# One encoder step on one core: attention groups written out, the softplus of both pairs of heads together, magnitudes on VectorE, last rows stored by quarters

## The chip, the core and the metric

The kernel runs on one core of a Trainium2 chip. The metric is the device time of one execution in microseconds (us). The core's engines are TensorE (PE: matmuls and transposes; PEld is its weight load), VectorE (DVE), ScalarE (ACT), GpSimd (POOL) and SyncE (SP), whose queue (SPq) starts most of the transfers. They run side by side and wait for each other through semaphores.

## The reference

```
layer 0: x = x + gate1 * (attention(norm(x)) @ w_o);   x = x + gate2 * swiglu(norm(x))
layer 1: x = x + gate1 * pool_mixer(norm(x));          x = x + gate2 * swiglu(norm(x))

z       = (q @ k.T) * HEAD_DIM ** -0.5                  # per head, strictly causal
ls_neg  = log_sigmoid(-z)                               # = -softplus(z)
log_1m  = where(causal, ls_neg, 0)
later   = cumsum(log_1m, reverse=True) - log_1m
weights = where(causal, exp(z + ls_neg + later), 0)
out     = weights @ v
```

There are 256 new frames of one prompt and 16 new frames of each of 8 running streams (384 tokens), a width of 2048, 16 heads of 128, 512 cached keys and values for each stream, a feed-forward width of 5632, and everything is in 32-bit floats. The changed code is attention in layer 0 and the last stage, which returns x as rows.

## The kernel before

The order of the work is written out by hand: each engine has its own program, and counting semaphores connect them. x lies in SBUF with features on partitions. The weights come in pieces of 1 MB. ACT and VectorE split each piece into a high and a low part, and TensorE makes three products of them (lines 1458 to 1460). This makes up nearly the whole kernel. Between the projections of q, k and v and the output projection stands attention.

Attention takes the heads in four groups of four. Each engine runs one loop over the groups. Within a group the heads form two pairs for the new frames' own scores ("self"), and the streams form two halves of four for the scores against the cache ("past"). A group goes so:

- TensorE turns q and k (line 1628), ACT copies qT, VectorE copies kT (line 1192), and TensorE makes the self scores of all four heads (lines 1722 to 1724).
- For each of the 8 streams b, TensorE turns the cached keys (`turn_keys(b)`, line 1639). ACT copies two heads of them and VectorE the other two (`keys_out(b)`, lines 761 and 1199). TensorE makes the past scores (`past_scores(b)`, line 1652), ACT copies them out (`scores_row(b)`, line 767), TensorE turns them back (`turn_scores(b)`, line 1660), and VectorE stores them (`scores_out(b)`, line 1205).
- In between, each self pair and each past half needs softplus(z) = max(z, 0) + log(1 + exp(-|z|)). ACT makes |z|, exp and log one after another in one buffer, `e_buf` (lines 744, 748, 750), and VectorE adds max(z, 0) (lines 1229 and 1252). Exp and log lie in different tables of ACT, and a change between them is an ACT_TABLE_LOAD. TensorE then sums along the keys with a triangular matrix (`self_sums`, line 1698; `past_sums`, lines 1667 and 1668), VectorE subtracts the sums, ACT takes exp, and TensorE multiplies with the values (`self_values`, `past_values`, line 1680). Past outputs leave through `out_row` (ACT, line 771) and `turn_out` (line 1687).

Each piece of the cache has one of four buffers. SP loads a new one when `turn_keys` or `past_values` has used the old one (line 371).

At the end of the kernel, after the last residual addition (lines 1046 to 1054), TensorE turns all of x with 48 transposes (line 1895). VectorE and ACT copy them into `yrow`, and SP stores it with three transfers (line 479).

Of the kernel before, what the change touches and what calls it, by code (L numbers as in the profile page):

```python
# [23 lines left out]
ALU = mybir.AluOpType  # L24
# [77 lines left out]
def encoder_step(nc, x_prompt, x_sample, c_prompt, c_sample, cache_k, cache_v, state_pool,  # L102
# [5 lines left out]
    with ctx:  # L108
# [76 lines left out]
        e_buf = at(R2 + 8192, "e_buf", [P, 2, 512])  # L185
        sp_buf = at(R2 + 12288, "sp_buf", [P, 2, 512])
# [8 lines left out]
        z_rows = [at(H0 + 14 * TOK * 4, "z_row0", [P, 512]), at(H0 + (KT + 14) * TOK * 4, "z_row1", [P, 512])]  # L195
# [30 lines left out]
        front_free, back_free, kturn_done, qkT_done, qT_ready, kT_ready = sem("front_free"), sem("back_free"), sem("kturn_done"), sem("qkT_done"), sem("qT_ready"), sem("kT_ready")  # L226
        zself_done, zself_taken = sem("zself_done"), sem("zself_taken")
# [54 lines left out]
        def unit(W, n):  # L282

            return W + n // 4, n % 4

# [33 lines left out]
        def _(sp):  # L319
# [155 lines left out]
            sp.wait_ge(y_act, 6)  # L475
            sp.wait_ge(y_dve, 6)
            for t in range(TT):
                dst = y_prompt[0, t * P:(t + 1) * P] if t < 2 else y_sample.rearrange("b t n -> (b t) n")
                sp.dma_start(dst, yrow[:, t]).then_inc(y_stored, 16)
            sp.wait_ge(y_stored, 16 * TT)  # L480
# [70 lines left out]
        def _(act):  # L551
# [189 lines left out]
            def softplus_step(z, i):  # L741

                if i == 0:
                    step.mark(act.activation(e_buf[:], z, ACT.Abs))
                    return
                act.wait_ge(act_step, step.value())
                if i == 1:
                    step.mark(act.activation(e_buf[:], e_buf[:], ACT.Exp, scale=-1.0))
                else:
                    act.activation(e_buf[:], e_buf[:], ACT.Ln, bias=1.0).then_inc(ln_ready, 1)  # L750

            with loop(act, 0, HG, {step: 8}) as g:
                act.wait_ge(qkT_done, g + 1)
# [19 lines left out]
                def self_rest(p, i):  # L773
                    if i == 0:
                        act.wait_ge(zself_taken, 2 * g + p + 1)
                        if p:
                            act.wait_ge(sp_ready, 4 * g + 1)
                    softplus_step(zs_self[:, 2 * p:2 * p + 2], i)

# [11 lines left out]
                def past_rest(q, i):  # L791
                    if i == 0:
                        act.wait_ge(zpast_taken, 8 * g + 4 * q + 4)
                        act.wait_ge(sp_ready, 4 * g + 2 + q)
                    softplus_step(half(zs_past, q), i)

# [15 lines left out]
                act.wait_ge(of_ready, g + 1)  # L812
                act.activation(h_hi[:, ds(g * 4, 4), PROMPT:TOK], o_f[:], ACT.Copy).then_inc(ofhi_ready, 1)
# [112 lines left out]
            for i in range(1, 12, 2):  # L926
                t, q = i % TT, i // TT
                act.wait_ge(yT_done, i + 1)
                act.activation(yrow[:, t, q * 512:(q + 1) * 512], bank[:, i % 6], ACT.Copy).then_inc(y_act, 1)
# [5 lines left out]
        def _(dve):  # L935
# [254 lines left out]
            with loop(dve, 0, HG, {step: 8}) as g:  # L1190
                dve.wait_ge(kturn_done, g + 1)
                dve.tensor_copy(kT[:], bank[:, 4:8, 0:TOK]).then_inc(kT_ready, 1)
# [22 lines left out]

                def self_scores(p):

                    dve.wait_ge(zself_done, g + 1)
                    pair = slice(2 * p, 2 * p + 2)
                    dve.scalar_tensor_tensor(zs_self[:, pair], bank[:, pair, :], SCALE, mask[:].unsqueeze(1).to_broadcast([P, 2, 512]),  # L1220
                                             ALU.mult, ALU.min).then_inc(zself_taken, 1)

                def self_sp(p):
# [5 lines left out]
                    dve.scalar_tensor_tensor(sp_buf[:], zs_self[:, 2 * p:2 * p + 2], 0.0, e_buf[:], ALU.max, ALU.add).then_inc(sp_ready, 1)  # L1229
# [40 lines left out]
                keys_out(0); self_scores(0)  # L1270
                keys_out(1); self_scores(1); self_sp(0)
# [12 lines left out]
                dve.wait_ge(opast_taken, 4 * g + 4)  # L1284
                own()
                dve.tensor_tensor(o_f[:], o_f[:], o_new[:], ALU.add).then_inc(of_ready, 1)
                dve.wait_ge(ofhi_ready, g + 1)
                k = ds(g * 4, 4)
                dve.tensor_tensor(h_lo[:, k, PROMPT:TOK], o_f[:], h_hi[:, k, PROMPT:TOK].bitcast(f32), ALU.subtract).then_inc(o_split, 1)
# [65 lines left out]

            def dense_chunk(W, c, r, last=False):
# [5 lines left out]
                for s in range(4):  # L1362
                    if not last:
                        dense(W, 12 + s)
                    down_add(4 * W + 9 + s, s, r, 1)

# [79 lines left out]
            for i in range(0, 12, 2):  # L1446
                t, q = i % TT, i // TT
                dve.wait_ge(yT_done, i + 1)
                dve.tensor_copy(yrow[:, t, q * 512:(q + 1) * 512], bank[:, i % 6]).then_inc(y_dve, 1)

# [4 lines left out]
        def _(pe):  # L1455
# [48 lines left out]
            def to_features(W, n, b0, act_h, act_l, k0, start, stop, second_half=None):  # L1504
# [3 lines left out]
                for k in range(4):  # L1508
                    if k == 2 and second_half:
                        pe.wait_ge(h_ready, second_half)  # L1510
# [111 lines left out]
            with pe.Fori(0, HG) as g:  # L1622
                pe.wait_ge(qk_loaded, 48 * g + 48)
                for i, free, done in ((0, front_free, qkT_done), (1, back_free, kturn_done)):
# [5 lines left out]
                    last.then_inc(done, 1)  # L1630

                def turn_keys(b):
                    pe.wait_ge(kv_loaded[b % 4], 64 * g + (16 * (b // 4) + 16))
                    for i, taken in ((0, keys_act), (1, keys_dve)):
                        if b:
                            pe.wait_ge(taken, 8 * g + b)
                        for h in (2 * i, 2 * i + 1):
# [80 lines left out]
                pe.wait_ge(kT_ready, g + 1)  # L1718
                turn_keys(0)
                pe.wait_ge(qT_ready, g + 1)  # L1720
                for h in range(4):
# [200 lines left out]
```

## Time and profile before

| | us |
|---|---|
| median of 3 runs | 3508.49 |
| lowest and highest run | 3506.6 and 3509.36 |
| the profiled execution's own time | 3510.57 |
| its span, first to last instruction | 3507.7 |

A profile comes from one execution, here one with 3507.7 us between its first and last instruction and 2.9 us around them. The page of the profile gives each engine's busy time. A window gives the same for a stretch, with the clock that TensorE was granted (1.00 is 2.4 GHz, 0.50 is 1.2 GHz). In a timeline the brackets hold the idle time before an instruction and what ended it.

### The profile page before, as it was taken

The page shows a single profiled execution, that of the slowest core. Times are in us where ns is not written, and L with a number is a line of the kernel's source. Part 1 is how long each engine was busy: PE and PEld are TensorE (multiplying, and loading weights), DVE is VectorE, ACT ScalarE, POOL GpSimd, SP SyncE. Part 2 cuts the span into 40 slices and gives each one's busy share as a digit, 9 for nine tenths or more (in the row PEclk, how much of TensorE's full clock was granted, in tenths as well). Part 3 has the DMA queues.
Part 4 walks back from the last instruction along what each step waited for, and adds up shares of the span by engine and source line. Part 5 has one row for each costly group of instructions (what it writes and reads, how often), then busy time and mean ns, then how long its engine had stood idle before and what let it go on. Part 6 is the DMA issues. An engine that isn't in the chain of part 4 may idle for free.

```text
span 3507.7 us, 48646 instructions
## 1 busy us (share of the span) xinstructions
PE 3316.0 (95%) x20405; PEld 2992.5 (85%) x20405; DVE 2076.4 (59%) x1782; ACT 1339.3 (38%) x1020; POOL 140.8 (4%) x141
## 2 busy tenths in 40 slices
PE   7999997887989999999999999878999999999998
PEld 4677775555978999999999999757999999999998
DVE  3487883444887777677776777675444443344443
ACT  3344444555444433444334443334222232322221
POOL 0000000000000000000000000010000000000000
PEclk9999998899999999999999999878999999999999
DMA  9776775676655555555555555463334333333331
GB/s 352 263 271 239 252 245 179 241 246 233 229 179 204 192 180 182 201 203 191 179 183 200 203 191 179 160 210 123 131 120 131 126 125 129 122 131 120 129 123 59
DMA packets 325244, 645.13 MB, mean 184 GB/s; under 512 B 11561, under 2 KB 14129, under 8 KB 324401
## 3 DMA queue, kind: packets, MB, share of 16 engines
q1 hardware_dynamic: 317984, 630.29, 52.6%
q10 hardware_dynamic: 7194, 13.91, 1.1%
q8 instruction: 47, 0.77, 0.1%
q14 instruction: 19, 0.16, 0.0%
HBM read 630.47 MB, written 13.69 MB: 184 GB/s over the span
## 4 chain that ended last, share of the span: by engine, by line
PE 86%; DVE 4%; DMA 4%; ACT 3%; issue 1%; SPq 1%; ACTq 0%; DVEq 0%
PE bank L1458 23%; PE bank L1460 22%; PE bank L1459 22%; PE bank L1537 3%; PE bank L1485 3%; PE bank L1539 3%; PE bank L1538 3%; DMA raw<-in_w_ada 3%; PE bank L1494 1%; PE bank L1667 1%; PE bank L1470 1%; PE bank L1639 1%; DVE w_lo L944 1%; PE bank L1668 1%; PE bank L1698 1%
## 5 line engine op out<-in xcount | busy, mean ns | idle before, releaser
L944 DVE TENSOR_TENSOR w_lo<-raw,w_hi 128x2048 fp32r<-128x2048 f32 x324 | 741.3, 2291 | 905.5 <-ACT w_hi L565 905.5
L565 ACT ACTIVATE w_hi<-raw 128x2048 fp32r<-128x2048 f32 x324 | 618.0, 1914 | 1379.9 <-PE bank L1460 1186.0
L1458 PE MATMUL bank<-h_hi,w_hi 128*128 128x384 f32 x3136 | 1064.2, 339 | 37.1 <-DVE h_lo L1023 23.3
L1460 PE MATMUL bank<-h_hi,w_lo 128*128 128x384 f32 x3136 | 1053.1, 336 | 0.0
L1459 PE MATMUL bank<-h_lo,w_hi 128*128 128x384 f32 x3136 | 1052.0, 335 | 0.0
L1458 PEld LDWEIGHTS bank<-h_hi,w_hi 128*128 128x128 f32 x3136 | 592.1, 189 | 83.0 <-issue 75.6
L1459 PEld LDWEIGHTS bank<-h_lo,w_hi 128*128 128x128 f32 x3136 | 592.4, 189 | 0.0
L1460 PEld LDWEIGHTS bank<-h_hi,w_lo 128*128 128x128 f32 x3136 | 591.7, 189 | 0.0
L1458 PE MATMUL bank<-act_hi,w_hi 128*128 128x384 f32 x1408 | 472.7, 336 | 0.0
L1460 PE MATMUL bank<-act_hi,w_lo 128*128 128x384 f32 x1408 | 470.5, 334 | 0.0
L1459 PE MATMUL bank<-act_lo,w_hi 128*128 128x384 f32 x1408 | 470.5, 334 | 0.0
L949 DVE TENSOR_TENSOR w_mid<-raw,w_top 128x2048 f32<-128x2048 f32 x144 | 329.0, 2285 | 11.5 <-ACT w_top L572 11.5
L951 DVE TENSOR_TENSOR w_top<-w_mid 128x2048 bf16<-128x2048 f32 x144 | 330.1, 2292 | 5.0
L572 ACT ACTIVATE w_top<-raw 128x2048 bf16<-128x2048 f32 x144 | 273.7, 1901 | 155.2 <-PE bank L1460 128.6
L1458 PEld LDWEIGHTS bank<-act_hi,w_hi 128*128 128x128 f32 x1408 | 264.3, 188 | 4.8 <-POOL act_lo L535 4.8
L1459 PEld LDWEIGHTS bank<-act_lo,w_hi 128*128 128x128 f32 x1408 | 264.3, 188 | 0.0
L1460 PEld LDWEIGHTS bank<-act_hi,w_lo 128*128 128x128 f32 x1408 | 264.3, 188 | 0.0
L535 POOL TENSOR_TENSOR act_lo<-act_f,act_hi 128x384 fp32r<-128x384 f32 x88 | 88.0, 1018 | 2728.7 <-ACT act_hi L839 2727.6
L1537 PE MATMUL bank<-w_hi,h_hi 128*128 128x512 f32 x480 | 192.5, 401 | 2.6 <-DVE w_lo L944 2.6
L1539 PE MATMUL bank<-w_hi,h_lo 128*128 128x512 f32 x480 | 187.8, 391 | 0.0
L1538 PE MATMUL bank<-w_lo,h_hi 128*128 128x512 f32 x480 | 187.6, 391 | 0.0
L1051 DVE SCALAR_TENSOR_TENSOR x<-bank,modT,x 128x256 f32<-128x256 f32 x384 | 158.4, 474 | 0.0
(219 smaller groups left out, 2564.8 us busy)
## 6 DMA issues: line engine op xcount, KB each, us to landing
raw<-in_w_ada SPq DMA_DIRECT2D x192, 1024.0 KB, 5.6
raw<-in_w_gate SPq DMA_DIRECT2D x88, 1024.0 KB, 5.2
raw<-in_w_up SPq DMA_DIRECT2D x88, 1024.0 KB, 5.2
raw<-in_w_down SPq DMA_DIRECT2D x88, 1024.0 KB, 5.1
raw<-in_w_qkv SPq DMA_DIRECT2D x40, 1024.0 KB, 5.2
raw<-in_cache_k SPq DMA_DIRECT2D x32, 1024.0 KB, 5.4
raw<-in_cache_v SPq DMA_DIRECT2D x32, 1024.0 KB, 6.8
raw<-in_w_o SPq DMA_DIRECT2D x16, 1024.0 KB, 5.0
```

Of the source, the lines that this page charges most:

```text
L565: act.activation(w_hi[:, s], raw[:, s], ACT.Copy).then_inc(hi_ready, 1)
L572: act.activation(w_top[:, s, 0], raw[:, s], ACT.Copy).then_inc(hi_ready, 1)
L944: dve.tensor_tensor(w_lo[:, s], raw[:, s], w_hi[:, s].bitcast(f32), ALU.subtract).then_inc(lo_ready, 1)
L949: dve.tensor_tensor(w_mid[:, s], raw[:, s], w_top[:, s, 0], ALU.subtract).then_inc(lo_ready, 1)
L951: dve.tensor_tensor(w_top[:, s, 1], w_mid[:, s], mid_top(s), ALU.subtract).then_inc(top_rest, 1)
L1051: step.mark(dve.scalar_tensor_tensor(xv, ps[:, k, 0:PROMPT], mod[:, k, 0:1], xv, ALU.mult, ALU.add))
L1458: pe.matmul(out, w, a, start=start, stop=False)
L1459: pe.matmul(out, w, al, start=False, stop=False)
L1460: return pe.matmul(out, wl, a, start=False, stop=stop)
L1537: pe.matmul(out, h_hi[:, kt, cols], w_hi[:, s, k], start=(kt == 0), stop=False)
L1538: pe.matmul(out, h_hi[:, kt, cols], w_lo[:, s, k], start=False, stop=False)
L1539: last = pe.matmul(out, h_lo[:, kt, cols], w_hi[:, s, k], start=False, stop=(kt == KT - 1))
```

## The change

1. The loops over the four groups are written out on TensorE, ACT and VectorE, so every wait names a constant.
2. kT is copied in two halves. The first starts when two heads' keys are turned, and turn_keys(0) waits for each half of the banks by itself. The self scores are signalled by pairs.
3. |z| is made on VectorE (`magnitude`), for the second self pair in a second buffer, `e_second`. ACT then takes exp of both self pairs and later log of both (`exp_part`, `log_part`).
4. TensorE does self_sums(0) after turn_scores(2) (it was after turn_scores(0)), self_sums(1) after turn_scores(3) (after turn_scores(2)), and past_sums(0) after past_scores(7) (before it).
5. A group's closing sum and split of the past outputs (`out_sum`, `out_lo`; on ACT `out_hi`) run at the start of the next group.
6. In the last chunk of the last feed-forward, the down projection makes x by quarters of 512 features. Each of the first three quarters is turned half-way through the next quarter's matmuls and the last one after the end. Each quarter is copied and stored by itself, so there are 12 stores of 256 KB instead of 3 of 1 MB.

```diff
-            with loop(act, 0, HG, {step: 8}) as g:
-                act.wait_ge(qkT_done, g + 1)
+            for g in range(HG):
+                act.wait_ge(qkT_done, 2 * g + 2)
                 act.activation(qT[:], bank[:, 0:4, 0:TOK], ACT.Copy).then_inc(qT_ready, 1)
...
+                def exp_part(i):
+
+                    e = e_second if i == 1 else e_buf
+                    act.wait_ge(abs_ready, 4 * g + i + 1)
+                    act.activation(e[:], e[:], ACT.Exp, scale=-1.0).then_inc(exp_ready, 1)
+
+                def log_part(i):
+
+                    e = e_second if i == 1 else e_buf
+                    act.wait_ge(exp_ready, 4 * g + i + 1)
+                    act.activation(e[:], e[:], ACT.Ln, bias=1.0).then_inc(ln_ready, 1)
...
-                keys_out(0); self_rest(0, 0); self_rest(0, 1)
-                keys_out(1); self_rest(0, 2); scores_row(0)
-                keys_out(2); scores_row(1); self_rest(1, 0)
-                keys_out(3); self_rest(1, 1); scores_row(2); self_rest(1, 2)
-                keys_out(4); scores_row(3)
-                keys_out(5); scores_row(4); self_w(0); past_rest(0, 0)
-                keys_out(6); past_rest(0, 1); scores_row(5); past_rest(0, 2)
-                keys_out(7); scores_row(6); scores_row(7); self_w(1); past_w(0)
-                past_rest(1, 0); past_rest(1, 1); past_rest(1, 2)
                 self_hi(0); out_row(0); past_w(1); self_hi(1); out_row(1)
...
+                keys_out(0); keys_out(1); exp_part(0)
+                scores_row(0); keys_out(2); exp_part(1)
+                scores_row(1); log_part(0); keys_out(3); log_part(1)
+                scores_row(2); keys_out(4)
+                scores_row(3); keys_out(5)
+                scores_row(4); self_w(0); exp_part(2); keys_out(6); log_part(2)
+                scores_row(5); keys_out(7)
+                scores_row(6); self_w(1); scores_row(7); past_w(0)
+                exp_part(3); log_part(3)
...
+            for g in range(HG):
+                for i in range(2):
+                    dve.wait_ge(kturn_done, 2 * g + i + 1)
+                    dve.tensor_copy(kT[:, 2 * i:2 * i + 2], bank[:, 4 + 2 * i:6 + 2 * i, 0:TOK]).then_inc(kT_ready, 1)
...
+                def magnitude(i):
+
+                    if i < 2:
+                        z, e = zs_self[:, 2 * i:2 * i + 2], (e_buf, e_second)[i]
+                        dve.wait_ge(zself_taken, 2 * g + i + 1)
+                    else:
+                        z, e = half(zs_past, i - 2), e_buf
+                        dve.wait_ge(zpast_taken, 8 * g + 4 * (i - 2) + 4)
+                        dve.wait_ge(sp_ready, 4 * g + (1 if i == 2 else 3))
+                    dve.scalar_tensor_tensor(e[:], z, -1.0, z, ALU.mult, ALU.max).then_inc(abs_ready, 1)
...
+                if g:
+                    out_sum(g - 1)
+                keys_out(0)
+                if g:
+                    out_lo(g - 1)
+                self_scores(0)
+                keys_out(1); magnitude(0); self_scores(1); magnitude(1)
                 keys_out(2); scores_out(0)
-                keys_out(3); self_t(0); scores_out(1); self_sp(1)
-                keys_out(4); scores_out(2)
-                keys_out(5); scores_out(3); self_t(1)
+                keys_out(3); scores_out(1); self_sp(0)
+                keys_out(4); scores_out(2); self_t(0); self_sp(1)
+                keys_out(5); scores_out(3); magnitude(2); self_t(1)
                 keys_out(6); scores_out(4); past_sp(0)
-                keys_out(7); scores_out(5); past_t(0); scores_out(6)
-                scores_out(7)
-                dve.wait_ge(o_split, g + 1)
+                keys_out(7); scores_out(5); past_t(0); scores_out(6); scores_out(7)
+                magnitude(3)
...
+            def rows_out(q):
+
+                for t in (0, 2):
+                    dve.wait_ge(yT_done, TT * q + t + 1)
+                    dve.tensor_copy(yrow[:, t, q * 512:(q + 1) * 512], bank[:, y_bank(q) + t]).then_inc(y_dve, 1)
...
-                turn_keys(2); past_scores(1); turn_scores(0); self_sums(0)
+                turn_keys(2); past_scores(1); turn_scores(0)
...
+            def turn_rows(q):
+
+                pe.wait_ge(residual_taken, R_END - 3 + q)
+                for t in range(TT):
+                    for k in range(4):
+                        last = pe.transpose(bank[:, y_bank(q) + t, k * P:(k + 1) * P], x[:, 4 * q + k, t * P:(t + 1) * P], ident[:])
+                    last.then_inc(yT_done, 1)
```

How the written order moves, at three places. First ACT in attention, from the second self pair's magnitude on (before): `e_buf<-zs_self` is |z|, `e_buf<-e_buf` after it is exp and then log, `z_row` is a copy of scores.

```order
L744 ACTIVATE e_buf<-zs_self 128x1024
L758 REGISTER_ALU
L761 ACTIVATE keys<-bank 128x1024
L746 REGISTER_ALU
L748 ACT_TABLE_LOAD
L748 ACTIVATE e_buf<-e_buf 128x1024
L764 REGISTER_ALU
L767 ACTIVATE z_row_109<-bank 128x512
L746 REGISTER_ALU
L750 ACT_TABLE_LOAD
L750 ACTIVATE e_buf<-e_buf 128x1024
L758 REGISTER_ALU
```

Now, from the first exp of a group on:

```order
L775 ACT_TABLE_LOAD
L775 ACTIVATE e_buf<-e_buf 128x1024
L765 ACTIVATE z_row_110<-bank 128x512
L759 ACTIVATE keys<-bank 128x1024
L775 ACTIVATE e_second<-e_second 128x1024
L765 ACTIVATE z_row_111<-bank 128x512
L781 ACT_TABLE_LOAD
L781 ACTIVATE e_buf<-e_buf 128x1024
L759 ACTIVATE keys<-bank 128x1024
L781 ACTIVATE e_second<-e_second 128x1024
```

|z| has left ACT, exp of one pair and exp of the other share one table, log of both shares the next, and key copies stand between them.

Second, TensorE in attention, from past_scores(1) on (before). `sp_buf,tri` and `sp_buf,ones` are self_sums, `ident,raw` is turn_keys, `keys,qT` is past_scores, `ident,z_row` is turn_scores.

```order
L1652 MATMUL bank<-keys,qT 32x512 x4
L1660 MATMUL bank<-ident,z_row_109 128x128 x4
L1692 ISA
L1696 REGISTER_ALU
L1698 MATMUL bank<-sp_buf,tri 128x512
L1699 MATMUL bank<-sp_buf,ones 128x128
L1698 MATMUL bank<-sp_buf,tri 128x512
L1699 MATMUL bank<-sp_buf,ones 128x128
L1636 REGISTER_ALU
L1639 MATMUL bank<-ident,raw 128x128 x16
```

Now, from turn_scores(2) on:

```order
L1692 MATMUL bank<-ident,z_row_110 128x128 x4
L1730 MATMUL bank<-sp_buf,tri 128x512
L1731 MATMUL bank<-sp_buf,ones 128x128
L1730 MATMUL bank<-sp_buf,tri 128x512
L1731 MATMUL bank<-sp_buf,ones 128x128
L1671 MATMUL bank<-ident,raw 128x128 x16
L1684 MATMUL bank<-keys,qT 32x512 x4
L1692 MATMUL bank<-ident,z_row_111 128x128 x4
L1730 MATMUL bank<-sp_buf,tri 128x512
L1731 MATMUL bank<-sp_buf,ones 128x128
```

Self_sums(0) stands two streams later, and self_sums(1) one stream after it.

Third, the end of TensorE's program. Before, where `ident,x` are the transposes of x:

```order
L1458 MATMUL bank<-act_hi,w_hi 128x384
L1459 MATMUL bank<-act_lo,w_hi 128x384
L1460 MATMUL bank<-act_hi,w_lo 128x384
L1884 REGISTER_ALU
L1884 COMPARE_AND_BRANCH
L1895 MATMUL bank<-ident,x 128x128 x48
```

Now, half-way through the last quarter's matmuls:

```order
L1486 MATMUL bank<-act_lo,w_hi 128x384
L1487 MATMUL bank<-act_hi,w_lo 128x384
L1860 MATMUL bank<-ident,x 128x128 x12
L1485 MATMUL bank<-act_hi,w_hi 128x384
L1486 MATMUL bank<-act_lo,w_hi 128x384
L1487 MATMUL bank<-act_hi,w_lo 128x384
```

The transposes of three quarters stand among the matmuls of the next quarter, 12 at each place, and 12 are left for the end.

## Rows read from the trace of the kernel before

**Rows 1.** the page's part on busy time: us, share of the span, instructions.

```profile
PE 3316.0 (95%) x20405; PEld 2992.5 (85%) x20405; DVE 2076.4 (59%) x1782; ACT 1339.3 (38%) x1020; POOL 140.8 (4%) x141
```

**Rows 2.** windows over attention: length, busy per engine, clock, DMA share, GB/s.

```profile
542.77:865.17 322.40, 259.83 (x2368) 179.30 (x2368) 132.46 (x183) 173.74 (x186) 0.00 (x0) 0.91 0.64 224
625.26:706.56 81.30, 65.70 (x592) 45.18 (x593) 33.60 (x47) 43.91 (x47) 0.00 (x0) 0.90 0.68 234
654.00:657.00 3.00, 1.09 (x9) 0.52 (x5) 1.34 (x2) 2.89 (x4) 0.00 (x0) 1.00 0.90 287
657.00:660.00 3.00, 3.00 (x6) 1.49 (x7) 1.64 (x3) 0.00 (x0) 0.00 (x0) 0.60 0.93 285
```

**Rows 3.** waits of PE in attention: total us, times, longest.

```profile
PE bank L1667 <- DVE later L1258: 16.0, 8, 3.0
PE bank L1639 <- ACT keys L761: 10.8, 8, 1.7
...
PE bank L1639 <- DVE kT L1192: 7.8, 4, 2.0
PE bank L1698 <- DVE sp_buf L1229: 7.6, 4, 1.9
```

**Rows 4.** ACT's groups in attention: busy us, mean ns, idle before.

```profile
L750 ACT ACT_TABLE_LOAD x16 | 20.5, 1283 | 0.3
L767 ACT ACTIVATE z_row<-bank 128x512 f32<-128x512 f32 x32 | 18.9, 590 | 37.2 <-PE bank L1652 37.2
...
L744 ACT ACTIVATE e_buf<-zs_self 128x1024 f32<-128x1024 f32 x8 | 8.4, 1052 | 21.1 <-DVE zs_self L1220 21.1
```

**Rows 5.** VectorE's groups in attention, same columns.

```profile
L1199 DVE COPY keys<-bank 128x1024 f32<-128x1024 f32 x32 | 39.1, 1222 | 44.2 <-PE bank L1639 44.2
...
L1258 DVE TENSOR_TENSOR later<-later,sp_buf 128x256 f32<-128x256 f32 x24 | 10.2, 425 | 0.8
```

**Rows 6.** timeline of the second group: start, us, engine, line, wait before.

```profile
628.13 1.76 DVE L1192 COPY kT<-bank 128x1536 f32<-128x1536 f32 x1
...
630.02 3.43 PE L1639 MATMUL bank<-ident,raw 128*128 128x128 f32 x16 [1.93 <-DVE kT L1192]
...
641.53 1.28 ACT L750 ACT_TABLE_LOAD   x1
...
641.57 1.97 PE L1639 MATMUL bank<-ident,raw 128*128 128x128 f32 x16 [1.67 <-ACT keys L761]
642.83 1.06 ACT L750 ACTIVATE e_buf<-e_buf 128x1024 f32<-128x1024 f32 x1
...
643.92 1.22 DVE L1229 SCALAR_TENSOR_TENSOR sp_buf<-zs_self,e_buf 128x1024 f32<-128x1024 f32 x1 [2.62 <-ACT e_buf L750]
...
644.52 1.06 PE L1652 MATMUL bank<-keys,qT 128*32 128x512 f32 x8 [0.98 <-ACT z_row L767]
...
675.23 2.08 PE L1667 MATMUL bank<-sp_buf,tri 128*128 128x512 f32 x2 [2.98 <-DVE later L1258]
```

**Rows 7.** timeline, the second half of the values' loads.

```profile
686.50 2.99 SPq L371 DMA_DIRECT2D raw<-in_cache_v  x4
```

**Rows 8.** the cache loads' line: from issue to landing.

```profile
DMA to landing us min/median/max: 4.9/5.6/12.9
```

**Rows 9.** timeline of the end.

```profile
3491.53 0.69 DVE L1054 TENSOR_TENSOR x<-x,tmp_s 128x512 f32<-128x512 f32 x1
...
3492.27 5.46 PE L1895 MATMUL bank<-ident,x 128*128 128x128 f32 x48 [3.08 <-DVE x L1054]
...
3497.77 0.60 ACT L929 ACTIVATE yrow<-bank 128x512 f32<-128x512 f32 x1 [0.28 <-PE bank L1895]
3498.43 1.79 SPq L479 DMA_DIRECT2D out<-yrow  x3
```

**Rows 10.** windows over the last feed-forward and the last stores.

```profile
2460.00:3489.00 1029.00, 1029.00 (x5938) 1028.88 (x5936) 421.00 (x419) 286.48 (x189) 40.29 (x40) 1.00 0.37 119
3499.00:3507.00 8.00, 0.00 (x0) 0.00 (x0) 0.00 (x0) 0.00 (x0) 0.00 (x0) 0.62 0.95 393
```

More of the change, by code:

```diff
@@ L194, in encoder_step @@
         keys = at(R1 + 47104, "keys", [P, 2, 4, 512])
-        z_rows = [at(H0 + 14 * TOK * 4, "z_row0", [P, 512]), at(H0 + (KT + 14) * TOK * 4, "z_row1", [P, 512])]
+        z_rows = [at(H0 + (KT + 12) * TOK * 4 + 2048 * i, f"z_row{i}", [P, 512]) for i in range(2)]
         o_row = at(R1 + 18432, "o_row", [P, 2, 512])
@@ L924, in _ @@
             dense_chunk(W_FFN1 + 3 * (CHUNKS - 1), 2 * CHUNKS - 1, last=True)
[L926 to L929, printed above, removed]
+            for q in range(4):
+                act.wait_ge(yT_done, TT * q + 2)
+                act.activation(yrow[:, 1, q * 512:(q + 1) * 512], bank[:, y_bank(q) + 1], ACT.Copy).then_inc(y_act, 1)
         @block.vector
@@ L1283, in _ @@
                 dve.memset(tmp_s[:, 0, 2:3], 0.0).then_inc(back_free, 1)
[L1284 to L1289, printed above, removed]
+            out_sum(HG - 1)
+            out_lo(HG - 1)
             own()
@@ L1365, in dense_chunk @@
                     down_add(4 * W + 9 + s, s, r, 1)
+                    if last:
+                        rows_out(s)
             with loop(dve, 0, CHUNKS - 1, {step: 4 * ADD}) as c:
@@ L1508, in to_features @@
                 for k in range(4):
+                    if k == 2 and rows_of is not None:
+                        turn_rows(rows_of)
                     if k == 2 and second_half:
@@ L1619, in _ @@
             ada_turn(ADA_O - 1, 7)
-            with pe.Fori(0, HG) as g:
+            for g in range(HG):
                 pe.wait_ge(qk_loaded, 48 * g + 48)
@@ L1629, in _ @@
                                                 tok[:, i, t, h * HD:(h + 1) * HD], ident[:])
-                    last.then_inc(done, 1)
+                        if h % 2:
+                            last.then_inc(done, 1)
                 def turn_keys(b):
@@ L1724, in _ @@
                     last = pe.matmul(bank[:, h, 384:512], kT[:, h, 2 * P:3 * P], qT[:, h, 2 * P:3 * P], start=True, stop=True)
-                last.then_inc(zself_done, 1)
+                    if h % 2:
+                        last.then_inc(zself_done, 1)
                 turn_keys(1); past_scores(0)
-                turn_keys(2); past_scores(1); turn_scores(0); self_sums(0)
+                turn_keys(2); past_scores(1); turn_scores(0)
                 turn_keys(3); past_scores(2); turn_scores(1)
-                turn_keys(4); past_scores(3); turn_scores(2); self_sums(1)
-                turn_keys(5); past_scores(4); turn_scores(3)
+                turn_keys(4); past_scores(3); turn_scores(2); self_sums(0)
+                turn_keys(5); past_scores(4); turn_scores(3); self_sums(1)
                 turn_keys(6); past_scores(5); turn_scores(4)
-                turn_keys(7); past_scores(6); turn_scores(5); past_sums(0)
-                past_scores(7); turn_scores(6); turn_scores(7)
+                turn_keys(7); past_scores(6); turn_scores(5)
+                past_scores(7); past_sums(0); turn_scores(6); turn_scores(7)
                 self_values(0)
@@ L1816, in mixed_chunk, with dense_chunk @@
                 down_rest(W, 16, r)
-            def dense_chunk(W, c, r, hr):
+            def turn_rows(q):
+                pe.wait_ge(residual_taken, R_END - 3 + q)
+                for t in range(TT):
+                    for k in range(4):
+                        last = pe.transpose(bank[:, y_bank(q) + t, k * P:(k + 1) * P], x[:, 4 * q + k, t * P:(t + 1) * P], ident[:])
+                    last.then_inc(yT_done, 1)
+            def dense_chunk(W, c, r, hr, last=False):
                 pe.wait_ge(residual_taken, r - 1)
@@ L1883, in _ @@
             norm_stats(3)
-            with pe.Fori(0, CHUNKS) as c:
+            with pe.Fori(0, CHUNKS - 1) as c:
                 dense_chunk(W_FFN1 + c * 3, c + CHUNKS, R_FFN1 + c * 4, 8)
-            for i in range(12):
-                t, q = i % TT, i // TT
-                if i == 0:
-                    pe.wait_ge(residual_taken, R_END)
-                if i >= 6:
-                    pe.wait_ge(y_act if i % 2 else y_dve, (i - 6) // 2 + 1)
-                for k in range(4):
-                    last = pe.transpose(bank[:, i % 6, k * P:(k + 1) * P], x[:, 4 * q + k, t * P:(t + 1) * P], ident[:])
-                last.then_inc(yT_done, 1)
+            dense_chunk(W_FFN1 + 3 * (CHUNKS - 1), 2 * CHUNKS - 1, R_FFN1 + 4 * (CHUNKS - 1), 8, last=True)
+            turn_rows(3)
 INPUTS = ["x_prompt", "x_sample", "c_prompt", "c_sample", "cache_k", "cache_v", "state_pool", "w_ada",
```

93 lines of the change are left out of this document (45 added, 48 removed).

## The prediction

> **What bounds the kernel now.** I read the page's busy times first. TensorE is busy 95% of the span [rows 1], so in most stages its matmuls set the end and only work taken from them counts. The page's slices show less in few places; attention is one. A window over it, from the first transpose of q to the last of the outputs, has 322.4 us with TensorE busy for 259.8 and a mean clock of 0.91 [rows 2]. So 62.6 us there are waits, and 0.09 x 2 x 322.4 = 58 us pass at 1.2 GHz, which costs up to half of itself, 29 us. Work at full clock is then 259.8 - 29 = 231 us, or 57.7 for each of the four groups; the group in the second row takes 81.3.
>
> The waits come next. The longest kinds are TensorE's for the past sums (16.0), for ACT's key copies (10.8), for kT (7.8) and for the self sums (7.6) [rows 3]. All but kT lead to ACT, which makes |z|, exp and log in one row with table loads: 16 loads stand before a log alone, each 1283 ns [rows 4]. The timeline shows how: ACT's load begins at 641.53 and its log at 642.83, VectorE's sum waits 2.62 for it, TensorE waits 1.67 for the key copy queued between them and 0.98 for the scores' copy; later it waits 2.98 for the past sums' operand [rows 6]. What the waits do to the clock is in two windows: in the 3 us from 654 TensorE is busy for 1.09 us, and in the next 3 the clock's mean is 0.60, at work all the time [rows 2].
>
> **The change, part by part.** ACT loses four |z| a group, 4 x 1.05 = 4.2 us [rows 4], and table loads: by the written order it has 9 a group before, and 7 in the first and 6 in the other groups now, so 11 fewer in all. A load costs ACT 1.28 and the log starts 0.02 after it ends [rows 6], so 11 are 14.3 us of ACT, some 3.6 a group. The Trainium skill (ScalarE: Activation LUTs, "What ACT_TABLE_LOAD costs") adds about 1.38 us of draining to each load, which would make 29 us of them; the rows show no such gap, so 14.3 stands. VectorE gains four magnitudes a group at the 1.22 us of its like [rows 6], 4.9 us, and it has room: busy 132 of 322 [rows 2].
>
> What counts is where TensorE still waits. I laid the new order out at full clock with the durations of the rows: 1.8 us to turn a stream's keys, 1.0 for its scores [rows 6], 1.22 for a key copy, 3 x 0.43 for the three additions of the past sums [rows 5], 0.59 for a scores' copy [rows 4], and 0.1 to 0.3 for each hand-over. Group two onwards:
> - turn_keys(0): 1.93 before [rows 6]. Half of kT takes an estimated 0.95 of the 1.76 and starts six transposes earlier: 0.7 now.
> - turn_keys(2) had 1.67 and now none, since exp stands behind both copies. But past_scores(1) waits for scores_row(0), behind a VectorE copy, a magnitude and an exp: 1.2 + 1.2 + 1.05 + 0.6 + 0.3 = 4.3 against TensorE's 2.8 of other work, so 1.5 (was 0.98).
> - turn_keys(4): keys_out(3) stands behind a load and a log: 0.8. The self sums, two streams later, find their operand long ready: none (was up to 1.9).
> - past_scores(7): VectorE copies its keys only after past_sp(0) and the three additions, 1.2 + 1.3 + 1.2 after the log, 0.3 of hand-overs: 2.0. The past sums behind it then find their operand: none (was 2.98).
> - turn_scores(7): waits for scores_out(6), behind past_t(0), which waits for the past sums: 1.45.
> - the end of the group has its old chain, shorter by one |z| on ACT: 0.9 + 1.2 + 0.7 + 0.9 = 3.7.
>
> The sum is 10.2 a group. The same laying-out of the old order gives 17.3 where the trace has 62.6 / 4 = 15.6, so I take the new one down alike, to 9.4: 6.2 a group, **25 us**. Written-out loops are costed at nothing: their register steps lie beside waits.
>
> The clock: the old group's 29 us in four groups are 7.2 each, or about four falls of some 3.4 us (13.6 us at half speed). In the trace a fall follows a wait near 2 us or two close together. The new list has two such places, past_scores(7) with 2.0 and the pair 0.9 + 1.2 around turn_out(0), both at the border. I take one fall a group, 1.7 us, and so 6.8 in all: **22 us** come back. The bounds are nothing back (0) and everything (29).
>
> The end: before, TensorE waits 3.08 until 3492.27, turns 48 blocks in 5.46 (0.114 each), the last copy begins at 3497.77, the stores at 3498.43 [rows 9], and the span ends at 3507.7. From the last matmul to the end that is 18.5 us. Now 36 transposes move in front of the last matmul, 36 x 0.114 = 4.1 us on TensorE. They don't wait: half of a quarter's 48 products takes 24 x 1029 / 5938 = 4.2 us [rows 10], the addition before them 3.1, cover 1.1; if it went, each of the three would cost what is missing. After the last matmul come 3.1 for the addition, 12 transposes 1.4, a hand-over and copy 1.0, and a store of 0.26 MB. The three old ones, 3.15 MB at 393 GB/s [rows 10], take 8.0 of the 9.3 us from their first start to the end, so 1.3 lies around a transfer, and the new last one takes 1.3 + 0.7 = 2.0, with 0.2 for its place in the queue. Sum: 4.1 + 3.1 + 1.4 + 1.0 + 2.2 = 11.8, **6.5 us** less. The bounds: 3.8 with the shortest landing of a 1 MB cache load, 4.9 [rows 8], in place of the last 2.2, and 6.7 with no place in the queue; 6.5 is nearer to what the last stores' own rows say. The Trainium skill (DMA: Bandwidth & Descriptors) gives a fixed part of about 2.0 us for a transfer; by it the gain would be 5.8, and the trace's own 1.3 is used.
>
> The transfers: attention moves 224 GB/s in the mean [rows 2], and the queue reaches 393 [rows 10], so a group at 69 us needs 224 x 80.6 / 69 = 262. Tight is one place: the last four pieces of the values start when past_values(0) to (3) are done, 686.50 to 689.5 [rows 7], and 4.2 MB at 393 need 10.7 + 1.3 = 12 us. TensorE asks for the last of them 2.8 + 1.5 + 1.2 + 3.4 + 1.9 + 0.7 + 2.8 = 14.3 us after the first is free. I cost this at nothing with 2 us of cover.
>
> Sum: 25 + 22 + 6.5 = 53.5. The profiled execution has 3510.6, so 3457.1. Its time is 2.1 above the median of the runs shown, so the median becomes 3508.5 - 53.5 = **3455.0**.
>
> **The rivals.**
> - The clock stays down (0.16). Shorter waits are still waits, and nine a group remain; if there are as many falls as before, 25 + 6.5 = 31.5 is gained: 3477. For it: two gaps are at the border. Against it: no gap is left near 3 us.
> - The transfers take part of it (0.14). The key and value buffers come free earlier, the queue is full after it, and landing takes up to 12.9 us under load against 4.9 [rows 8]. If each group waits 3 us for its last values or the next group's first keys, 12 us are lost: 3467. Against it: the 2 us of cover above.
> - All of the clock comes back, none of the gaps reaches the border (0.10): 3508.5 - 25 - 29 - 6.5 = 3448.
> - Slower (0.03): the written-out programs are fetched once for each group, through the engines that carry the cache. If a fetch lands late, as the cache loads do under load (12.9 [rows 8]), and TensorE, strictly in order, stands still at it, each costs up to 12.9. It decides from 53.5 / 4 = 13.4 us a group, just over one such stop; with two in each group it is 103 - 53.5: 3558. Against it: the stage before attention is already written out, and none of TensorE's waits there is put down to anything but data.
> - The change doesn't do what it says (0.02): a new wait as long as each old one, a group again 81 us, and only the end gains: 3502.
>
> **How the numbers follow.** The forecast has 0.55. Its own range is 3446 to 3464, from the gaps (9.4 give or take 1.5 a group, 6 us) and one fall more or less in two groups (3). The range for 8 times in 10 reaches over the clock's two bounds, 3448 and 3477, and the transfers: 3444 to 3478. This kernel can tell a change of about 0.2%, 7 us, from none. All cases but the slower one and a part of the last lie below 3501.5: faster 0.94, same 0.02, slower 0.04.
>
> **What the profile after would show.** Right: attention from first to last transpose near 274 us (322.4 before), TensorE's waits in it near 38, its mean clock above 0.96, 25 table loads in it, no wait for self_sums or past_sums(0), the longest waits at past_scores(1), past_scores(7) and turn_scores(7), and 12 us from the last matmul to the end. Wrong: waits of TensorE for a transfer or for nothing that is named, a clock still at 0.91, or a wait of turn_rows inside the last quarters.

## The result and the profile after

| | before | after |
|---|---|---|
| median, us | 3508.93 (4 runs, 3506.6 to 3510.11) | 3454.73 (4 runs, 3454.09 to 3463.35) |
| profiled execution / its span | 3510.57 / 3507.7 | 3454.09 / 3452.4 |

The ratio is 0.985, with a 95% interval of 0.9838 to 0.9862; the forecast was 3455.0, and 3457.1 for the profiled execution. The two traces, cut into four stages (us):

| stage | before | after | difference | forecast |
|---|---|---|---|---|
| start to attention | 542.8 | 541.0 | -1.8 | 0 |
| attention | 322.4 | 273.7 | -48.7 | -47 |
| to the last matmul's end | 2624.0 | 2628.7 | +4.6 | +4.1 |
| from there to the end of the span | 18.5 | 9.1 | -9.4 | -10.6 |

The first row is no work of the change: in the runs below, whose code before attention is the changed kernel's, this stage is 540.0 to 543.3 us long. Windows over attention, over its second group, over a wait in it and over the stretch behind that, after (columns as in [rows 2]):

```profile
540.99:814.65 273.66, 236.00 (x2368) 169.39 (x2368) 151.65 (x203) 145.16 (x160) 0.00 (x0) 0.98 0.74 265
609.99:679.16 69.17, 57.75 (x594) 41.24 (x593) 38.28 (x52) 36.09 (x40) 0.00 (x0) 1.00 0.82 291
675.30:677.50 2.20, 0.00 (x0) 0.00 (x0) 0.00 (x0) 0.00 (x0) 0.00 (x0) 1.00 0.92 339
679.80:683.20 3.40, 3.40 (x18) 3.40 (x17) 0.59 (x3) 1.45 (x1) 0.00 (x0) 0.50 1.06 392
```

The same 2368 matmuls keep TensorE busy for 236.0 instead of 259.8 us, which is the clock (a mean of 0.98 instead of 0.91), and 37.7 us of waits are left of 62.6. TensorE's waits in attention, after:

```profile
PE bank L1657 <- DMA tok<-out: 6.5, 1, 6.5
PE bank L1684 <- DVE keys L1212: 6.4, 4, 1.6
PE bank L1719 <- ACT o_row L769: 6.1, 8, 0.8
PE bank L1692 <- DVE zs_past L1218: 5.2, 4, 1.3
PE bank L1684 <- ACT z_row L765: 4.9, 4, 1.2
PE bank L1699 <- DVE later L1282: 4.0, 4, 1.0
PE bank L1712 <- ACT zs_past L795: 3.0, 4, 0.7
PE bank L1671 <- ACT keys L759: 2.8, 4, 0.7
PE bank L1712 <- issue: 2.3, 1, 2.3
PE bank L1671 <- DMA raw<-in_cache_k: 1.7, 2, 1.0
PE bank L1712 <- DMA raw<-in_cache_v: 0.9, 2, 0.6
PE bank L1671 <- DVE kT L1205: 0.2, 1, 0.2
```

The first row ends before the attention window's first matmul and is not in the 37.7. Against [rows 3]: the past sums fell from 16.0 to 4.0, the key copies by ACT from 10.8 to 2.8, kT from 7.8 to 0.2, and no row for the self sums is left. New are the waits for VectorE's keys and stored scores, for the cache's transfers, and one that names nothing ("issue", 2.3). Its place, in TensorE's timeline after:

```profile
674.33 0.95 PE L1712 MATMUL bank<-raw,zs_past 128*32 128x128 f32 x25 [0.31 <-DMA raw<-in_cache_v]
677.54 0.42 PE L1712 MATMUL bank<-raw,zs_past 128*32 128x128 f32 x7 [2.26 <-issue]
678.67 0.66 PE L1719 MATMUL bank<-ident,o_row 128*128 128x128 f32 x4 [0.71 <-ACT o_row L769]
679.16 4.45 PE L1657 MATMUL bank<-ident,tok 128*128 128x128 f32 x24
```

Seven matmuls from the end of the second group's values TensorE stands still for 2.26 us; then the clock falls (the last window above) and 24 transposes take 4.45 us. It falls once more, in the fourth group. The waits that stand before that fall, and the windows over the stretch behind them in the first and the fourth group:

```profile
596.41 0.66 PE L1719 MATMUL bank<-ident,o_row 128*128 128x128 f32 x4 [0.82 <-ACT o_row L769]
598.07 1.13 PE L1699 MATMUL bank<-sp_buf,tri 128*128 128x512 f32 x2 [1.01 <-DVE later L1282]
800.02 0.66 PE L1719 MATMUL bank<-ident,o_row 128*128 128x128 f32 x4 [0.82 <-ACT o_row L769]
801.69 1.18 PE L1699 MATMUL bank<-sp_buf,tri 128*128 128x512 f32 x2 [1.01 <-DVE later L1282]
598.00:602.00 4.00, 3.93 (x11) 2.02 (x12) 1.14 (x4) 0.00 (x0) 0.00 (x0) 1.00 1.05 393
802.50:806.00 3.50, 3.50 (x5) 1.35 (x4) 0.07 (x1) 0.00 (x0) 0.00 (x0) 0.52 1.06 392
```

In all four groups TensorE waits 0.82 us for ACT's outputs there and then 1.01 for the past sums; only in the fourth does the clock fall behind them. ACT's table loads in attention, after, are 12 + 8 + 4 + 1 = 25, as forecast:

```profile
L781 ACT ACT_TABLE_LOAD x12 | 15.4, 1283 | 0.2
L786 ACT ACT_TABLE_LOAD x8 | 10.3, 1283 | 0.1
L795 ACT ACT_TABLE_LOAD x4 | 5.1, 1283 | 0.1
L775 ACT ACT_TABLE_LOAD x1 | 1.3, 1283 | 0.0
```

The end after, and the row of the stores (count, KB each, median us from issue to landing):

```profile
3446.38 1.53 PE L1860 MATMUL bank<-ident,x 128*128 128x128 f32 x12 [3.08 <-DVE x L1053]
3447.07 0.69 DVE L1384 COPY yrow<-bank 128x512 f32<-128x512 f32 x1 [0.75 <-PE bank L1860]
3447.95 0.69 DVE L1384 COPY yrow<-bank 128x512 f32<-128x512 f32 x1 [0.18 <-PE bank L1860]
```

```profile
out<-yrow SPq DMA_DIRECT2D x12, 256.0 KB, 3.0
```

12 transposes stand where 48 stood [rows 9], behind the same 3.08. From the end of the last copy, 3448.64, to the end of the span are 3.76 us. TensorE has no wait for x in the quarters before.

### The profile page after: what moved, and what is told of

It is laid out like the page before. It is cut to its first block, busy times and chain, and to the rows that moved or that the text cites. A ratio compares the mean times of both kernels' runs of the same rounds, so it can differ in the third digit from the quotient of the medians.

```text
span 3452.4 us, 48339 instructions
## 1 busy us (share of the span) xinstructions
PE 3289.4 (95%) x20405; PEld 2982.7 (86%) x20405; DVE 2097.3 (61%) x1804; ACT 1308.3 (38%) x991; POOL 140.7 (4%) x141
## 4 chain that ended last, share of the span: by engine, by line
PE 87%; DMA 5%; DVE 4%; ACT 2%; issue 1%; SPq 1%; DVEq 0%; ACTq 0%
PE bank L1485 23%; PE bank L1487 23%; PE bank L1486 23%; PE bank L1566 3%; DMA raw<-in_w_ada 3%; PE bank L1512 3%; PE bank L1568 3%; PE bank L1567 3%; PE bank L1671 1%; PE bank L1521 1%; DVE w_lo L943 1%; PE bank L1497 0%; DMA raw<-in_cache_k 0%; PE bank L1699 0%; DMA early_raw<-in_w_qkv 0%
```

## The experiments

Each run stood beside runs of the kernel before on its own chip; these went from 3503.0 to 3513.2 us in all, so effects of a few us are read from attention's length in the traces, one of each kernel. There the kernel before has 322.4 and the changed one 273.7. Such a length has two parts. TensorE's waits repeat: the kernel of experiment 2, whose attention is that of the kernel before, has the same sums of them to 0.1 us. Its busy time doesn't: 256.3 us against 259.8 for the same matmuls, as the clock falls at other places. So of an effect below, the part in the waits is firm and the part in busy time is known to some 3.5 us only.

**1. Only the loops written out** (kernel before, all three group loops; TensorE's is shown).

```diff
-            with pe.Fori(0, HG) as g:
+            for g in range(HG):
```

> The kernel before with only its group loops on TensorE, ACT and VectorE written out. My theory (the waits come from ACT's softplus chain, not from the loops): the same waits in every group, 15.6 us of them, attention 322 us less 0 to 3, total 3505 to 3509. Rival A (the written-out form is the gain: register steps, the table load at the loop's head): attention falls by 15 us or more, total under 3494. Rival B (fetching written-out code costs): a wait of TensorE that no data explains, 2 us or more, and a total above 3509.

3508.82 us, ratio 0.9995 (0.9986 to 1.0005), attention 322.2. TensorE's waits in it:

```profile
PE bank L1667 <- DVE later L1258: 15.6, 8, 2.8
PE bank L1639 <- ACT keys L761: 12.8, 8, 3.0
...
PE bank L1639 <- DVE kT L1192: 7.5, 4, 1.9
PE bank L1698 <- DVE sp_buf L1229: 7.3, 4, 1.8
...
PE bank L1680 <- issue: 5.2, 3, 3.1
```

Writing out gains nothing: every wait of [rows 3] is there within 2 us. It brings three waits that name nothing, in the past values, where before has none. All waits are 67.4 us for 62.6, and a busy time of 254.8 for 259.8 makes up for them.

**2. Only the end** (kernel before with part 6 of the change).

```diff
+            def turn_rows(q):
...
+                for t in range(TT):
+                    for k in range(4):
+                        last = pe.transpose(bank[:, y_bank(q) + t, k * P:(k + 1) * P], x[:, 4 * q + k, t * P:(t + 1) * P], ident[:])
```

> The kernel before with only the end changed (rows turned between the last quarters, 12 stores). If the parts add up: 5.3 us less, as the two traces differ from the last matmul on (18.5 against 9.1, with 4.1 us of transposes moved ahead), so 3503 to 3504, and attention stays at 322. Rival: moving 36 transposes ahead of the last matmul also costs waits inside the last quarters; then less than 4 us are gained.

3502.24 us, ratio 0.9981 (0.9972 to 0.9991). The last two stages are 2628.7 and 8.9 us, so the end gives 5 us alone as in the whole. Attention, which the edit doesn't touch, kept its waits (past sums 16.0, key copies 10.8, kT 7.8) and was 318.9: its waits are the same 62.6 us, and TensorE is busy for 256.3.

**3. TensorE's group loop kept** (changed kernel).

```diff
-            for g in range(HG):
+            with pe.Fori(0, HG) as g:
```

> The changed kernel with TensorE's group loop a loop again (ACT and VectorE stay written out). Theory: order and ACT decide, so attention stays within 3 us of 273.7. Rival (fetching TensorE's written-out code cost the unexplained 2.3 us wait in the second group, and the clock fall behind it): that wait goes, attention is 270 to 272, and the page shows fewer instruction packets than 66. A third way: the loop's branch costs something at each of three turns, and attention is longer by more than 3 us.

3451.58 us, ratio 0.984 (0.9823 to 0.9856). The window over attention:

```profile
543.29:810.67 267.38, 232.61 (x2368) 166.82 (x2368) 151.52 (x203) 145.14 (x160) 0.00 (x0) 0.99 0.77 270
```

6.3 us less than the changed kernel, 2.9 of them in waits and 3.4 in TensorE's busy time (the clock falls at neither place where it did). The named waits are the same within 0.4 us each, and the one with no name is gone. So that wait belongs to the written-out code of TensorE; that all of the 3.4 does is not shown. The totals alone don't part the two kernels clearly (3449.9 to 3455.3 against 3454.1 to 3463.4). The page's DMA queue for instructions moves 52 packets here and 66 in the changed kernel.

**4. |z| back on ACT**, at the head of `exp_part` (changed kernel).

```diff
...
+                    act.activation(e[:], z, ACT.Abs).then_inc(abs_ready, 1)
                     act.wait_ge(abs_ready, 4 * g + i + 1)
                     act.activation(e[:], e[:], ACT.Exp, scale=-1.0).then_inc(exp_ready, 1)
...
-                keys_out(1); magnitude(0); self_scores(1); magnitude(1)
+                keys_out(1); self_scores(1)
...
```

> The changed kernel with |z| back on ACT, at the head of exp_part; all orders and the paired softplus stay. Laid out at full clock, TensorE's wait at past_scores(1) shrinks from 1.5 to 0.2, those at turn_keys(4) and past_scores(6) grow by 0.9 and 0.9: +0.7 us a group, so +3 us in all: attention 275 to 279. Rival (taking |z| off ACT is the main gain of the change, 4.2 us of ACT a group on the path): attention at 288 us or more.

3460.4 us, ratio 0.9859 (0.9843 to 0.9876), attention 279.4. The waits for ACT's keys rise from 2.8 to 6.5, and from the second group on the wait for ACT's scores moves from past_scores(1) to past_scores(6), both as laid out. Moving |z| is worth about 6 us of the 48.7, 4.2 of them in waits; I expected 3.

**5. kT in one copy** (changed kernel).

```diff
-                for i in range(2):
...
+                dve.wait_ge(kturn_done, 2 * g + 2)
+                dve.tensor_copy(kT[:], bank[:, 4:8, 0:TOK]).then_inc(kT_ready, 2)
```

> The changed kernel with kT copied whole again, after all keys are turned. Theory: turn_keys(0) waits about 1.5 us more in each group, so attention is 6 us longer plus up to 5 us for falls of the clock at a wait of 2 us: 280 to 285 against 273.7. Rival (the halves do nothing because something else is late there): 273 to 276.

3462.51 us (one run), attention 281.3. The wait for kT is 8.1 us, against 0.2 with the halves and 7.8 in the kernel before. The halves are worth 7.6 us, 7.0 of them in waits.

**6. past_sums(0) before past_scores(7) again** (changed kernel).

```diff
-                turn_keys(7); past_scores(6); turn_scores(5)
-                past_scores(7); past_sums(0); turn_scores(6); turn_scores(7)
+                turn_keys(7); past_scores(6); turn_scores(5); past_sums(0)
+                past_scores(7); turn_scores(6); turn_scores(7)
```

> The changed kernel with past_sums(0) before past_scores(7) again, as in the kernel before, on TensorE alone. Laid out at full clock, the past sums wait 0.9, past_scores(7) nothing (1.6 now), turn_scores(7) 0.8 less: 1.8 us less a group, attention 7 us less, 265 to 268. Rival (this move was part of the gain, as the change has it): the 2.98 us wait before the past sums comes back and attention is 280 or more.

3446.09 us, ratio 0.9816 (0.9799 to 0.9832), attention 268.3. Its waits:

```profile
PE bank L1699 <- DVE later L1282: 5.7, 8, 1.0
...
PE bank L1692 <- DVE zs_past L1218: 2.4, 4, 0.6
```

The wait for the eighth stream's keys (6.4) is gone and that for the stored scores halved, for 1.7 us at the past sums. The waits fall by 6.0 us and the busy time rises by 0.6, so this part of the change costs 5.4 us: the wait that it avoids had shrunk from 2.98 to 0.41 (second group) by the other parts.

**7. The first magnitude ahead of VectorE's second key copy** (changed kernel).

```diff
-                keys_out(1); magnitude(0); self_scores(1); magnitude(1)
+                magnitude(0); self_scores(1); keys_out(1); magnitude(1)
```

> The changed kernel with VectorE's magnitude(0) and self_scores(1) ahead of keys_out(1), in time in which VectorE waits for the turned keys. Laid out: past_scores(1) waits no more (1.2 now) and turn_keys(4) 0.5 less, 2 us a group: attention 265 to 268. Rival (the cache's transfers take back what the order gives): attention 270 or more, with waits of TensorE for raw of 6 us or more (2.6 now).

3451.85 us (one run), attention 270.3: a miss. The waits went as laid out (ACT's scores 4.9 to 0.3, its keys 2.8 to 1.2), but TensorE was busy 238.6 us instead of 236.0, at a mean clock of 0.96 instead of 0.98. Its waits are 31.8 us instead of 37.7 (length less busy time); of these 5.9 us, 2.6 went back to the clock, which falls at three places here. The rival's sign, waits for the cache of 6 us or more, isn't there either (2.7). With 2.6 us inside what the busy time varies by, and one run, why the clock took them stays open.

**8. Both, 6 and 7** (changed kernel, the two edits above).

> Both of the last two together, on the changed kernel. Laid out: 3.8 us a group less, 15 in all, 258.5; with transfers that land as before and groups of 64 us, I expect 2 to 6 us of new waits for the values' and keys' pieces: attention 258 to 264, total 3439 to 3446. Rival (transfers bound it): attention above 266.

3445.57 us, ratio 0.9814 (0.9798 to 0.9831), attention 263.6, clock 0.96, the unnamed wait 2.3. Attention is 10.0 us shorter than in the changed kernel, where 6 and 7 alone gave 5.4 and 3.3.

**9. Self sums one stream earlier** (changed kernel).

```diff
-                turn_keys(3); past_scores(2); turn_scores(1)
-                turn_keys(4); past_scores(3); turn_scores(2); self_sums(0)
-                turn_keys(5); past_scores(4); turn_scores(3); self_sums(1)
+                turn_keys(3); past_scores(2); turn_scores(1); self_sums(0)
+                turn_keys(4); past_scores(3); turn_scores(2); self_sums(1)
+                turn_keys(5); past_scores(4); turn_scores(3)
```

> The changed kernel with both self sums one stream earlier on TensorE: after turn_scores(1) and turn_scores(2). ACT and VectorE keep their orders. Theory (the softplus chain is long, and the change hides it by asking for it later): the operands are late again; laid out at full clock, waits of 2.0 and 3.1 us there and 1.4 after them against 0.8 saved, 6.4 a group, so 25 us, and falls of the clock after them 5 to 10: attention 298 to 310. Rival (pairing exp and log is what matters, the place of the sums not): attention under 282.

3484.94 us (one run), attention 302.7. Its first waits:

```profile
PE bank L1730 <- DVE sp_buf L1253: 17.7, 8, 2.8
PE bank L1684 <- ACT z_row L765: 8.5, 8, 1.2
```

29 us, the largest effect of any single edit, for one step back of the two that the change moved self_sums(0) and the one that it moved self_sums(1). Nearly in their old place they wait 17.7 us, where the old orders on ACT and VectorE had them wait 7.6 [rows 3]: the new orders make their operand later, and the move of the sums hides that. Even without it attention stays 19.7 us shorter than in the kernel before.

**10. 8 with TensorE's group loop kept.**

> The version with magnitude(0) early and past_sums(0) back, with TensorE's group loop a loop again. The single effects on attention were -3.3, -5.4 (-10.1 together) and -6.3 for the loop. If they add: 263.6 - 6.3 = 257 for attention, total 3437 to 3441. If the loop only moved where the clock falls: 260 to 264, total as the written-out version, 3443 to 3446.

3438.65 us (5 runs), ratio 0.98 (0.9787 to 0.9813), faster than both kernels and, run for run, than experiment 8 (3436.6 to 3439.3 against 3443.6 to 3445.8). Window over attention, and waits:

```profile
542.61:800.17 257.56, 236.44 (x2368) 167.48 (x2368) 152.22 (x203) 144.73 (x160) 0.00 (x0) 0.98 0.80 280
```

```profile
PE bank L1719 <- ACT o_row L769: 6.1, 8, 0.8
PE bank L1699 <- DVE later L1282: 5.7, 8, 1.0
...
PE bank L1671 <- DMA raw<-in_cache_k: 1.6, 2, 1.1
```

Attention is as long as the single effects add up to (257 expected), and again no wait is without a name.

**11 and 12. What the unnamed wait is made of** (changed kernel; in 11 half, in 12 a sixteenth part of each cached tile is loaded, 64 KB of 1 MB; the rest of a tile keeps older data). What I wrote down for 12 says a thirty-second part and 32 KB, which is wrong: the edit takes one of four pieces and 128 of its 512 columns.

```diff
-                sp.dma_start(raw[:, j % 4], src[:, :, ahead:][:, :, ds(col, 512)]).then_inc(kv_loaded[j % 4], 16)
+                sp.dma_start(raw[:, j % 4, 0:2], src[:, 0:2, ahead:][:, :, ds(col, 512)]).then_inc(kv_loaded[j % 4], 16)
```

```diff
-                sp.dma_start(raw[:, j % 4], src[:, :, ahead:][:, :, ds(col, 512)]).then_inc(kv_loaded[j % 4], 16)
+                sp.dma_start(raw[:, j % 4, 0:1, 0:128], src[:, 0:1, ahead:][:, :, ds(col, 128)]).then_inc(kv_loaded[j % 4], 16)
```

> The changed kernel, with only the first two of four pieces of each cached key and value tile loaded (the other half of each tile keeps older data), so the cache's bytes halve and nothing else moves. Theory A, that TensorE's unnamed wait in the past values (2.3 us, 1 place, with the transfer engines busy 0.92 of that stretch) is the next piece of its written-out code arriving late behind the cache transfers: the waits for the cached tiles (1.7 + 0.9 us) go and the unnamed wait falls below 1 us; with the clock fall behind it gone too, attention goes from 273.7 to 266 to 270 us. Theory B, that the wait for the code has nothing to do with the transfers: the waits for the tiles go, the unnamed wait stays at 2 us or more, attention 270 to 272 us.

> The changed kernel, with a thirty-second part (32 KB instead of 1 MB) of each cached key and value tile loaded, at the same places of SyncE's program; the rest of each tile keeps older data. With half of the bytes the unnamed wait was still 2.25 us, at the same instruction, but the transfer engines were still 0.93 busy there. Now they are nearly idle for the whole of attention. Theory A, TensorE's written-out code comes late only when it has to share the transfer engines: the unnamed wait falls under 0.5 us or goes, the clock fall behind it goes, attention 264 to 268 us, as with TensorE's group loop kept (267.4, less the 1.6 + 0.8 us of waits for the tiles there). Theory B, the wait is the price of the written-out code itself at this place, where 7 instructions in a row are issued every 0.03 us: 2 us or more stay with idle transfer engines, attention 269 to 272 us.

3451.35 and 3453.16 us (one run each), attention 271.5 in both. In 11 the place still had the transfer engines 0.93 busy, so it could not decide; 12 did. Its timeline at the place, and the windows over most of the wait and over attention:

```profile
677.60 0.42 PE L1712 MATMUL bank<-raw,zs_past 128*32 128x128 f32 x7 [2.26 <-issue]
```

```profile
675.20:677.20 2.00, 0.14 (x5) 0.00 (x0) 0.00 (x0) 0.00 (x0) 0.00 (x0) 1.00 0.26 68
542.67:814.17 271.50, 235.13 (x2368) 169.27 (x2368) 151.59 (x204) 145.16 (x160) 0.00 (x0) 0.98 0.15 50
```

The same 2.26 us, at the same matmul, with the transfer engines 0.26 busy. Theory A falls: the wait is not the cache's transfers in the way of the code. Those two kernels lose the waits for tiles (2.6 us, of which the wait for kT takes back 1.3) and 0.9 us of busy time, so the transfers cost the changed kernel 2.2 us in all.

## Why the prediction was right, and where it was not

The three terms measured 24.9 us (waits), 23.8 (clock) and 4.8 (end) where 25, 22 and 6.5 were forecast. That both sums are 53.5 is luck: the clock's error and the end's cancel.

- **The waits that are named: right in place, 15% too long.** The longest were to be at past_scores(7), past_scores(1) and turn_scores(7), and are: 1.6 for 2.0, 1.2 for 1.5, 1.3 for 1.45. turn_keys(4) has 0.7 for 0.8, the self sums and past_sums(0) none. turn_keys(0) has at most 0.2 for kT where 0.7 was forecast, but there the cached keys come later still; without their transfers it has 0.5 (experiment 12). All named waits but the transfers' are 32.6 us, 8.1 a group, where the forecast took 9.4. As laid out, 10.2, it was 25% too long. Taking it down "alike", by 15.6 / 17.3, gives 9.2 and not 9.4, a slip of 0.8 us in all.
- **The transfers and the code: costed at nothing, and 4.9 us.** 1.7 and 0.9 for cached keys and values, 2.3 unnamed. The prediction names waits of both kinds as signs of being wrong, and both came. This and the error above cancel: 37.7 us of waits against 38 is better than the working deserved. The 2 us of cover at the values held almost everywhere (longest wait 0.6); the next group's first keys were the tighter place (1.0), and I hadn't laid that out.
- **The clock: right, 23.8 us for 22.** Attention starts at the low clock in both kernels (to about 546.7 in the changed one). Later it fell behind the unnamed wait and once more near 802, two falls for the four of the forecast. Of the two places called borderline, past_scores(7)'s 1.6 had no fall, and the pair around turn_out(0), 0.82 and 1.01, had one in four groups. The estimate of one fall a group was high; a fall that nothing in the working foresaw, at 680, made up part of it. And 1.8 us is less than the 3.5 by which the busy time of the kernel before's attention varies (experiment 2), so a hit this close is partly luck.
- **The slower rival was no fancy.** Of the rival on written-out code the wait is real (experiments 1, 3 and 10) and the size was far off: 2.3 us, about 1.7 for the fall of the clock behind it (3.4 us at half speed), and at most 6.3 in all, where it needed 53.5. My argument against it, that the stage before attention is written out and has no such wait, didn't transfer to the past values. Nor did its mechanism hold as I gave it: late behind the cache's bytes (experiment 12).
- **The end: 4.8 us for 6.5.** The two stages after attention give +4.6 and -9.4, against +4.1 and -10.6. The working has two slips here: its terms sum to 11.8, which is 6.7 below 18.5 and not 6.5, and the 11.8 includes the 4.1 before the last matmul, so its sign "12 us from the last matmul to the end" should have been 7.7; measured are 9.1. The last store was mis-sized: 2.2 forecast, 3.76 measured, with a median landing of 3.0 for stores of this size. The three old stores lay behind each other, so their 9.3 us around 8.0 of bytes showed a transfer's fixed part only where it wasn't hidden. A landing of 3.0 less 0.7 for the bytes at 393 GB/s leaves an estimated 2.3 around a transfer. The Trainium skill (DMA: Bandwidth & Descriptors, "Anatomy of one DMA", on transfers that GpSimd starts; these are SyncE's) has about 2.0 us fixed. That is nearer than the 1.3 read from the trace: the gain estimated by it was 5.8. The addition (3.08), the 12 transposes and the cover of the three moved blocks came as laid out.
- **Table loads: right.** 25, at 1283 ns each. No more than 0.4 us of idle time in all stands before them, so the draining that was left out of the sum isn't there after either.
- **The parts, one by one.** Undoing one costs 29 (place of the self sums, 23.4 of it waits), 7.6 (kT), 5.7 (|z|), and gives 5.4 (place of past_sums(0)) and 6.3 (TensorE's loop). The rest isn't shared out: the new order of exp and log with its 11 table loads fewer, and the closing work moved to the next group (part 5), were not undone alone. The effects don't simply add either, as experiment 9 shows (17.7 us of waits where the old orders had 7.6).

Open stays what the unnamed wait is. Shown is that it comes with TensorE's loop written out and goes when it is kept (no such wait in the traces of before, 2, 3 and 10), that it stands at the same seven last matmuls of the second group's past values in experiments 4 to 9, 11 and 12 (0.9 to 2.9 us), and that it is 2.26 us with the cache's bytes and with a sixteenth of them. That it is the fetch of code is the natural reading of the packets on the instruction queue; no run shows it directly.

## What to carry to other kernels

When an in-order engine waits in many places, lay the new order out between all engines with measured durations, and do it for each part of the change by itself: two parts here (past_sums(0), TensorE's loop written out) cost 5 to 6 us of attention each, clock included, and were carried by the rest. A reordering that was made against a wait should be tried again once the wait is short. Price the last transfer of a kernel by the landing of one of its own size, not by a row of stores that hide each other.

## What was not expected of the hardware

- In the written-out stream TensorE stood still for 0.2 to 3.1 us with no wait for data that the profile shows, only among the past values, matmuls issued every 0.03 us. In the other stages of attention, with matmuls of 0.1 us and more, the same code showed no such wait.
- What waits cost in clock can't be read from their lengths alone. In the changed kernel the waits of 0.82 and 1.01 us stand in each of the four groups, and the clock fell behind them once. In the 69 us of the second group up to 679.16, with its 1.6 at past_scores(7), the clock's mean is 1.00. The kernel before and that of experiment 2 have the same waits in attention, and 259.8 and 256.3 us of busy time. What decides it is not shown here.
